# Second score pass over 128 rows, and the last norm with tokens on the partitions

## The reference

```python
def rms_norm(x, g):
    y = x * lax.rsqrt(jnp.mean(x * x, axis=-1, keepdims=True) + EPS)
    return y * g

def stick_breaking_attention(q, k, v):          # 8 heads of 64 channels
    for i in range(S // BLOCK_Q):                # blocks of 128 queries
        z = jnp.einsum('bhqd,bhkd->bhqk', qs, kk) * scale
        log_keep = jnp.where(mask, jax.nn.log_sigmoid(-z), 0.0)
        suffix = lax.cumsum(log_keep, axis=3, reverse=True) - log_keep
        a = jnp.where(mask, jnp.exp(jax.nn.log_sigmoid(z) + suffix), 0.0)
        outs.append(jnp.einsum('bhqk,bhkd->bhqd', a, vv))

def reference(x, ...):
    for l in range(DEPTH):                       # DEPTH = 2
        x = x + hybrid_mixer(x, ...)             # attention above, retention, gates, w_o
        x = x + conv_ffn(x, ...)
    return rms_norm(x, final_norm)
```

## Time and profile before

| | us |
|---|---|
| median of 3 runs | 1654.8 (1654.22 to 1655.73) |
| the profiled execution | 1654.76 |
| its span, from the first to the last instruction | 1652.9 |

### The profile page before, as it was taken

The page is one execution under the profiler, slowest core; times in us unless marked ns, Lnnn a source line. Parts: engine busy times, 40 slices in busy tenths (PEclk is TensorE's granted clock), DMA queues, the critical chain, the costliest instruction groups (busy, mean ns, idle before and its releaser), DMA issues.

```text
span 1652.9 us, 19423 instructions
## 1 busy us (share of the span) xinstructions
PE 1634.0 (99%) x7390; PEld 1351.0 (82%) x7390; DVE 943.6 (57%) x1108; ACT 638.6 (39%) x747; POOL 168.8 (10%) x157
## 2 busy tenths in 40 slices
PE   9999999999999999999999999999999999999996
PEld 7888888888888888888888888888888888888885
DVE  7268865566665566524253787645666656565223
ACT  5244334323345444522233533333333554444211
POOL 4001220000310000002200112200005000000021
PEclk9999999999999999999999999999999999999998
DMA  5332222222332323233233222232222223232321
GB/s 189 102 115 77 77 77 89 71 71 91 100 92 99 101 90 102 90 101 98 93 102 114 90 78 77 79 96 68 77 91 100 93 98 100 90 102 92 100 100 66
DMA packets 44107, 154.43 MB, mean 93 GB/s; under 512 B 4928, under 2 KB 5056, under 8 KB 44048
## 3 DMA queue, kind: packets, MB, share of 16 engines
q1 hardware_dynamic: 41904, 148.39, 27.5%
q10 hardware_dynamic: 1872, 4.33, 1.0%
q0 software_dynamic: 272, 0.85, 0.1%
HBM read 149.36 MB, written 2.10 MB: 92 GB/s over the span
## 4 chain that ended last, share of the span: by engine, by line
PE 97%; DVE 1%; DMA 0%; POOL 0%; ACT 0%; issue 0%; DVEq 0%; SPq 0%; POOLq 0%
PE ps L831 30%; PE ps L833 30%; PE ps L832 30%; PE ps L921 1%; PE ps L910 1%; PE ps L945 1%; PE ps L899 1%; PE ps L895 1%; PE ps L953 1%; PE ps L941 1%; DMA w_raw<-wts 0%; PE ps L1039 0%; PE ps L932 0%; DVE gate L821 0%; DVE rinv L818 0%; PE ps L877 0%
## 5 line engine op out<-in xcount | busy, mean ns | idle before, releaser
L831 PE MATMUL ps<-u_hi,w_hi 128*128 128x512 f32 x1344 | 530.4, 395 | 0.0
L833 PE MATMUL ps<-u_hi,w_lo 128*128 128x512 f32 x1344 | 523.6, 390 | 0.0
L832 PE MATMUL ps<-u_lo,w_hi 128*128 128x512 f32 x1344 | 523.0, 389 | 0.0
L559 DVE TENSOR_TENSOR w_lo<-w_raw,w_hi 128x1024 fp32r<-128x1024 f32 x275 | 353.4, 1294 | 289.2 <-ACT w_hi L378 285.4
L378 ACT ACTIVATE w_hi<-w_raw 128x1024 fp32r<-128x1024 f32 x275 | 288.0, 1055 | 289.4 <-DMA w_raw<-wts 283.1
L833 PEld LDWEIGHTS ps<-u_hi,w_lo 128*128 128x128 f32 x1344 | 252.3, 188 | 53.5
L831 PEld LDWEIGHTS ps<-u_hi,w_hi 128*128 128x128 f32 x1344 | 252.4, 188 | 53.2 <-issue 0.5
L832 PEld LDWEIGHTS ps<-u_lo,w_hi 128*128 128x128 f32 x1344 | 252.5, 188 | 51.7 <-issue 0.5
L831 PE MATMUL ps<-g_hi,w_hi 128*128 128x512 f32 x352 | 136.9, 389 | 0.0
L832 PE MATMUL ps<-g_lo,w_hi 128*128 128x512 f32 x352 | 136.9, 389 | 0.0
L833 PE MATMUL ps<-g_hi,w_lo 128*128 128x512 f32 x352 | 136.9, 389 | 0.0
(11 more groups left out here) (162 smaller groups left out, 1935.9 us busy)
## 6 DMA issues: line engine op xcount, KB each, us to landing
w_raw<-wts SPq DMA_DIRECT2D x275, 512.0 KB, 3.4
x<-xt SPq DMA_DIRECT2D x8, 256.0 KB, 7.2
q<-q ACTq DMA_DIRECT2D x8, 256.0 KB, 3.6
out<-gate SPq DMA_DIRECT2D x6, 256.0 KB, 2.9
dec<-decay ACTq DMA_DIRECT2D x2, 514.0 KB, 4.4
cs<-rope ACTq DMA_DIRECT2D x2, 512.0 KB, 3.8
w_raw<-wts SPq DMA_DIRECT2D x2, 256.0 KB, 4.3
out<-gate POOLq DMA_DIRECT2D x2, 256.0 KB, 3.0
```

The lines of the kernel that those rows point to most:

```text
L559: nc.vector.tensor_tensor(w_lo[:, s, :], w_raw[:, s, :], w_hi[:, s, :].bitcast(F32), ALU.subtract).then_inc(s_lo, 1)
L831: nc.tensor.matmul(dst, a_hi, b_hi, start=start, stop=False)
L832: nc.tensor.matmul(dst, a_hi, b_lo, start=False, stop=False)
L833: return nc.tensor.matmul(dst, a_lo, b_hi, start=False, stop=stop)
```

## The change

Two independent things.

The second score pass runs over 128 rows. `q_lo` becomes four tiles of 128 partitions x 2 heads x 512. Each head's low part is written to its own half of the partitions as before (line 745, now at the place `q_lo[p][b:b + 64, b // 64, :]`), and the other half holds zeros, so what it multiplies in `k2` (k's low part) adds nothing. POOL writes the zeros by four memsets in each layer, and DVE waits for them before it writes into a tile (`s_qz`). The tiles lie in parts of memory that other data use at other times, so `warm` moves too.

The last norm has tokens on the partitions. x times gain goes to `xg` (for k 0 to 3 on ACT during the last slabs, for 4 to 7 on DVE as each x is ready). PE transposes `xg` in 32 blocks of 128x128 into PSUM, four to a piece; a piece is 128 tokens x 512 channels. The sum of squares is now taken by matmuls with one column, four for `ssum`, into which POOL has added a third square, and four for the last square, so the sum stands as one column of four numbers per partition. Root and reciprocal are over 128x4 (`rcol`), and DVE and ACT in turn scale the eight pieces out of PSUM by a number per partition into `rows`. SP writes all eight, 256 KB each, in rows of 2 KB to an output whose rows are 4 KB. The host no longer transposes.

The diff:

```diff
@@ -79,7 +79,7 @@
 GR_TILE, GATE_TILE = 16, 24
 SILU_AT = 42
 SIGMOID_AT = {46: range(0, 10), 51: range(10, 16)}
-DVE_OUT = 6
+PIECES = [(0, 0), (1, 0), (2, 0), (3, 0), (1, 1), (2, 1), (3, 1), (0, 1)]
 EARLY = 2
 HALF = SLAB // 2
 WARM_UP = 8
@@ -120,8 +120,12 @@
 
         K = 1024
         x = sb("x", [P, KT, S], F32)
+        u_hi_at = at[0]
         u_hi = sb("u_hi", [P, KT, S], F32R)
+        xg = sb("xg", [P, KT, S], F32, u_hi_at)
+        u_lo_at = at[0]
         u_lo = sb("u_lo", [P, KT, S], F32R)
+        rows = sb("rows", [P, TT, D], F32, u_lo_at)
         w_hi = sb("w_hi", [P, RING, SLAB], F32R)
         ring_at = at[0]
         w_raw = sb("w_raw", [P, RING, SLAB], F32)
@@ -145,7 +149,8 @@
         TMP = M + 112 * K
         q2 = sb("q2", [P, SB_HEADS, S], F32R, QK)
         k2 = sb("k2", [P, SB_HEADS, S], F32R, G_)
-        q_lo = sb("q_lo", [P, SB_PAIRS, S], F32R, G_ + 22 * K)
+        q_lo = [sb(f"q_lo{p}", [P, 2, S], F32R, (SG_ + 12 * K, TMP + 5 * K, G_ + 22 * K, G_ + 26 * K)[p])
+                for p in range(SB_PAIRS)]
         qk_tmp = sb("qk_tmp", [P, 2, S], F32, SG_ + 8 * K)
         osb = sb("osb", [P, SB_PAIRS, 2, S], F32R, QK)
         otmp = sb("otmp", [P, S], F32, G_ + 30 * K)
@@ -179,7 +184,7 @@
         cb_at = M + 88 * K + 8 * (S + 8)
         cb = sb("cb", [P, 2, S], F32, cb_at)
         cc = sb("cc", [P, 2, S], F32, cb_at + 4 * K)
-        warm = sb("warm", [P, 512], BF16, TMP + 5 * K)
+        warm = sb("warm", [P, 512], BF16, G_ + 8 * K)
         sq = sb("sq", [P, S], F32, TMP)
         ssum = sb("ssum", [P, S], F32, TMP + 2 * K)
         assert TMP + 9 * K <= nc.sbuf_usable_end, (TMP + 9 * K, nc.sbuf_usable_end)
...
@@ -303,10 +310,13 @@
                 for i in range(SLABS // RING * RING, SLABS):
                     sp.wait_ge(s_free, l * SLABS + i + 1)
                     load(l, i % RING, i)
-            for k in range(DVE_OUT):
-                sp.wait_ge(s_fin, k + 1)
-                sp.dma_start(out[k], gate[:, k, :]).then_inc(s_out, 16)
-            sp.wait_ge(s_out, 16 * DVE_OUT)
+            for n, (tt, h) in enumerate(PIECES):
+                if n % 2 == 0:
+                    sp.wait_ge(s_find, n // 2 + 1)
+                else:
+                    sp.wait_ge(s_fina, n // 2 + 1)
+                sp.dma_start(out[tt, :, h * 512:h * 512 + 512], rows[:, tt, h * 512:h * 512 + 512]).then_inc(s_out, 16)
+            sp.wait_ge(s_out, 16 * len(PIECES))
 
         @block.gpsimd
         def _(pool):
@@ -342,6 +352,8 @@
             for l in range(DEPTH):
                 if l > 0:
                     sum_squares(l * 30, lambda k: l * TILES + k + 1)
+                for p in range(SB_PAIRS):
+                    nc.gpsimd.memset(q_lo[p][:].bitcast(F32), 0.0).then_inc(s_qz, 1)
                 for h in range(SB_HEADS):
                     pool.wait_ge(s_beta, l * 8 + h + 1)
                     for c in range(TT):
@@ -355,19 +367,10 @@
                     nc.gpsimd.tensor_tensor(rstd[:, 1, :], rstd[:, 0, :], halff, ALU.pow).then_inc(s_rs, 1)
                 sum_squares(l * 30 + 15, lambda k: l * TILES + TILE_CREDIT + WO_TILE + k + 1)
             sum_squares(DEPTH * 30, lambda k: DEPTH * TILES + k + 1, 4)
-            for k in (4, 5):
+            for k in (4, 5, 6):
                 pool.wait_ge(s_fsq, k - 3)
                 pool.wait_ge(s_sq, DEPTH * 30 + 3 + k)
                 nc.gpsimd.tensor_tensor(ssum[:], ssum[:], gate[:, KT + k, :], ALU.add).then_inc(s_sq, 1)
-
-            pool.wait_ge(s_gx, KT - DVE_OUT)
-            pool.wait_ge(s_r, DEPTH * 3 + 1)
-            for k in range(DVE_OUT, KT):
-                nc.gpsimd.tensor_tensor(gate[:, k, :], gate[:, k, :], rinv[:], ALU.mult).then_inc(s_finp, 1)
-            for k in range(DVE_OUT, KT):
-                pool.wait_ge(s_finp, k - DVE_OUT + 1)
-                pool.dma_start(out[k], gate[:, k, :]).then_inc(s_outp, 16)
-            pool.wait_ge(s_outp, 16 * (KT - DVE_OUT))
 
         @block.scalar
         def _(act):
@@ -544,11 +547,22 @@
                         for k in range(EARLY):
                             act.wait_ge(s_tile, l * TILES + TILE_CREDIT + DOWN_TILE + k + 1)
                             u_high(k, pcol(l + 1, PAR_ATTN + k))
+            nc.scalar.activation(rcol[:, 0:1], epsf, ACT.Sqrt)
+            for k in range(4):
+                act.wait_ge(s_tile, DEPTH * TILES + k + 1)
+                nc.scalar.activation(xg[:, k, :], x[:, k, :], ACT.Copy,
+                                     scale=pars[:, DEPTH * NPAR + k:DEPTH * NPAR + k + 1]).then_inc(s_xga, 1)
             for k in range(4, KT):
                 act.wait_ge(s_tile, DEPTH * TILES + k + 1)
                 nc.scalar.activation(gate[:, KT + k, :], x[:, k, :], ACT.Square).then_inc(s_fsq, 1)
             act.wait_ge(s_nrm, DEPTH * 3 + 1)
-            nc.scalar.activation(rinv[:], ps[:, 4, :], ACT.Sqrt, bias=epsf, scale=1.0 / D).then_inc(s_rt, 1)
+            nc.scalar.activation(rcol[:], ps[:, 0, 0:TT], ACT.Sqrt, bias=epsf, scale=1.0 / D).then_inc(s_rt, 1)
+            act.wait_ge(s_r, DEPTH * 3 + 1)
+            for n, (tt, h) in enumerate(PIECES):
+                if n % 2 == 1:
+                    act.wait_ge(s_xt, n + 1)
+                    nc.scalar.activation(rows[:, tt, h * 512:h * 512 + 512], ps[:, tt + 4 - 4 * h, :], ACT.Copy,
+                                         scale=rcol[:, tt:tt + 1]).then_inc(s_fina, 1)
 
         @block.vector
         def _(dve):
@@ -573,6 +587,12 @@
                 dve.wait_ge(s_oh, l * 8 + h + 1)
                 nc.vector.tensor_tensor(osb[b:b + 64, p, 1, :], otmp[b:b + 64, :], osb[b:b + 64, p, 0, :].bitcast(F32),
                                         ALU.subtract).then_inc(s_ol, 1)
+
+            def gained(k):
+
+                dve.wait_ge(s_tile, DEPTH * TILES + k + 1)
+                nc.vector.tensor_scalar(xg[:, k, :], x[:, k, :], pars[:, DEPTH * NPAR + k:DEPTH * NPAR + k + 1], None,
+                                        ALU.mult).then_inc(s_xgd, 1)
 
             def last_tile(l):
 
@@ -740,7 +760,9 @@
                                 for b in (0, 64):
                                     h = 2 * p + b // 64
                                     hi = (q2, k2)[j % 2][b:b + 64, h, :]
-                                    lo = q_lo[b:b + 64, p, :] if j % 2 == 0 else k2[64 - b:128 - b, h, :]
+                                    lo = q_lo[p][b:b + 64, b // 64, :] if j % 2 == 0 else k2[64 - b:128 - b, h, :]
+                                    if j % 2 == 0:
+                                        dve.wait_ge(s_qz, l * SB_PAIRS + p + 1)
                                     dve.wait_ge(s_qh, l * 16 + 4 * j + 2 * t + b // 64 + 1)
                                     nc.vector.tensor_tensor(lo, qk_tmp[b:b + 64, t, :], hi.bitcast(F32), ALU.subtract).then_inc(s_ql, 1)
                         if kind == "yb":
@@ -806,20 +828,21 @@
                                 slab_done(l, i)
                             nc.vector.tensor_tensor(x[:, 4 * q + t, :], x[:, 4 * q + t, :], ps[:, 4 - 4 * q + t, :],
                                                     ALU.add).then_inc(s_tile, 1)
+                            if q == 1 and l + 1 == DEPTH:
+                                gained(4 + t)
                         if q == 0 and l + 1 < DEPTH:
                             for t in range(EARLY):
                                 u_low(l * 16 + 16, t, pcol(l + 1, PAR_ATTN + t))
             last_tile(DEPTH)
-            for k in range(DVE_OUT, KT):
-                dve.wait_ge(s_tile, DEPTH * TILES + k + 1)
-                nc.vector.tensor_scalar(gate[:, k, :], x[:, k, :], pars[:, DEPTH * NPAR + k:DEPTH * NPAR + k + 1], None,
-                                        ALU.mult).then_inc(s_gx, 1)
+            gained(KT - 1)
             dve.wait_ge(s_rt, DEPTH * 3 + 1)
-            nc.vector.reciprocal(rinv[:], rinv[:]).then_inc(s_r, 1)
+            nc.vector.reciprocal(rcol[:], rcol[:]).then_inc(s_r, 1)
             dve.wait_ge(s_r, DEPTH * 3 + 1)
-            for k in range(DVE_OUT):
-                nc.vector.scalar_tensor_tensor(out=gate[:, k, :], in0=x[:, k, :], scalar=pars[:, DEPTH * NPAR + k:DEPTH * NPAR + k + 1],
-                                               in1=rinv[:], op0=ALU.mult, op1=ALU.mult).then_inc(s_fin, 1)
+            for n, (tt, h) in enumerate(PIECES):
+                if n % 2 == 0:
+                    dve.wait_ge(s_xt, n + 1)
+                    nc.vector.tensor_scalar(rows[:, tt, h * 512:h * 512 + 512], ps[:, tt + 4 - 4 * h, :], rcol[:, tt:tt + 1], None,
+                                            ALU.mult).then_inc(s_find, 1)
 
         @block.tensor
         def _(pe):
@@ -885,7 +908,7 @@
 
             def scores(l, h):
 
-                b, p = 64 * (h % 2), h // 2
+                p = h // 2
                 pe.wait_ge(s_ql, l * 16 + (6, 8, 14, 16)[p])
                 pe.wait_ge(s_qd[p // 2], l * 32 + 32)
                 if h == 0:
@@ -896,8 +919,8 @@
```

(42 more changed lines are left out.)

5 lines of the change are left out of this document (1 added, 4 removed).

## The result

The kernel after takes 1646.72 us (median of 5 runs, 1645.74 to 1647.29), the kernel before 1654.8 (5 runs, 1654.22 to 1655.93): a ratio of 0.9946 [0.9935, 0.9957], 8.1 us less. The forecast of 1645.1 has the direction right and lies 1.6 us low, inside its range of 1643.0 to 1649.5.

The account below looks back on a forecast made before the run. TensorE (PE), on the chain for 97% of the 1652.9 us span, was taken as the bound, with DMA at the end. Padding 5.2 plus end 4.5 makes 9.7 off 1654.8: 1645.1 us, own range 1643.4 to 1647, stated range 1643.0 to 1649.5.

Parts of the forecast that it names:

- The pauses: Padded second score pass: 6.4 us saved over 16 heads, less 0.8 at head 2 and 0.4 at head 3, leaves 5.2.
- the 0.40 a head: PE's scoring of each head: shorter steps and first matmuls at both borders of the second pass save 0.39, called 0.40 us.
- The steps into and out of the pass: PE at the second pass's borders: 0.26 becomes 0.12 going in, 0.25 becomes 0.12 going out, saving 0.14 and 0.13 us.
- the followers: First matmul of the pass and first weight matmul behind it: each goes from 0.34 to 0.28 us, saving 0.06.
- head 3: PE waits for DVE's sp_lo, whose chain begins with the sigmoid behind the scoring: 0.2 us lost, 0.4 in two layers.
- The end: Rebuilt last norm: first output 2.7 us earlier, then DMA bound, end of the span 4.5 us earlier; bounds 2.5 and 4.9.
- The 0.36 for POOL and DVE: Last residual adds: DVE's multiplies and POOL's adds make each other wait, releasing POOL's third add 0.36 us later; bounds 0, 1.4.
- The signs named for a right forecast: Line 922 0.12 behind line 918; 0.8 wait at head 2; root near 1634.8; eight issues within 4 us; DMA share 1.0.
- A: Scoring pauses come from the other operand or the bank, not the rows, and stay: 1650.3 us; chance 0.10.
- B: The end gives half: multiplies push back POOL's third add and SP's single queue doesn't fill the DMAs; 1647.1 us, chance 0.11.
- C: Output transfers in halves of 4 KB rows run at half DMA rate: 5.6 us more, 1650.7 us; chance 0.03.
- D: POOL's zeros slow, DVE queues behind them: memsets over 20 us begin to cost, at 24 the time is 1662.1; chance 0.02.

Follow-up runs that it names:

- alternate_64: The kernel before with the two score passes of a head alternating matmul by matmul, the second still over 64 rows; 1671.78 us.
- late_gain: The kernel after with DVE's four multiplies by the gain behind the last residual add instead of between the adds; 1646.37 us.
- alternate_128: The kernel before with only the padded second pass, the two passes alternating matmul by matmul, both over 128 rows; one run, 1651.21 us.
- part two: The kernel after with q_lo and the 64-row second pass as in before, so only the last norm is changed; 1651.55 us.
- two_queues: The kernel after with ScalarE issuing the output transfers of its own four pieces and SP only the others; 1646.69 us.
- combined: The kernel after with the changes of reorder and short_end together; 1644.52 us.
- short_end: The kernel after with POOL adding two squares, PE summing tiles 6 and 7, one piece transposed before the sums, late gain multiplies, ScalarE's piece first; 1645.17 us.
- again: The kernel after, unchanged, run and profiled once more; 1646.99 us.
- part one: The kernel before with only the padded q_lo, its memsets and the second pass over 128 rows; 1650.69 us.
- reorder: The kernel after with ScalarE's sigmoids before w_hi and DVE's scan before w_lo in the sixteen scoring slabs; 1645.57 us.
- both combined: Two kernels: combined, 1644.52 us, and combined with ScalarE issuing the output transfers of its own pieces, 1644.2 us.

## Why the prediction was right

**The pauses (5.2 forecast, 4.66 measured).** The mechanism and the 0.40 a head hold: 0.39 in each of 16 heads, 6.27 in sum. That the 0.40 came out is luck in part, by two errors that cancel. The steps into and out of the pass save 0.09 and not 0.14 and 0.13, since with 128 rows they are 0.17 and not 0.12; the followers save 0.10 each and not 0.06, since they hold their place 0.235 or near it. I had priced the quicker followers as an alternative (0.50 a head) and not taken it.

The mis-sized term is head 3: "the half saved after it (0.2) is lost". The whole 0.4 is lost. I let the chain start with the scoring, and in fact ScalarE was behind. The rows for it were in the trace of before (984.88 for the end of PE's last scoring matmul, 984.96 for the sigmoid, with `w_hi` ending at 984.93), and I didn't read them. In two layers this costs 0.4 more than forecast. The 4.66 has two further parts that the forecast knew nothing of: 0.41 lost ahead of the first scoring, and 0.45 gained in small steps between and behind the scorings, which I can't put down to anything. With them, 6.27 less 0.82 at head 2, less 0.83 at head 3, less 0.41, plus 0.45 is 4.66. From the first scoring to T alone 5.07 us are gained. That this is near 5.2 is luck too.

Of the two rules of the Trainium skill, the rows side at the borders with the one that a change of tiling mode drains TensorE ("TensorEngine Tiling (Array Packing)", section Key Properties): alternate_64 prices a border at 0.18 us. That it is a drain no row shows. The rule that a matmul over few rows takes as long as one over 128 ("TensorE: Matmul & The Clock Gate", section "Why this matters for your kernels") holds between borders: within the pass the second and third matmul hold their places 0.179 and 0.060 us with 64 rows, 0.174 and 0.061 with 128.

**The end (4.5 forecast, 4.5 measured).** Here also two terms moved against each other. The 0.36 for POOL and DVE was charged to the wrong side: POOL's adds took 1.28 to 1.30 throughout, and the multiplies were held up, 0.93, 0.80 and 0.84 instead of 0.48, each ending 0.28 behind POOL's add (1630.29 behind 1630.00). DVE's residual adds came 0.2 to 0.3 late, of which 0.05 reached POOL's third add (T + 0.70, and T + 0.65 in late_gain). So the root came 0.30 earlier than forecast. That was given back behind it: DVE's first piece starts 0.26 behind DVE's own reciprocal (ScalarE's starts 0.04 behind it, 1635.48 to 1635.52) and takes 0.75, not 0.69. The first output came at T + 5.6 as forecast, and from there to the end of the span it was 7.2 us, as forecast, with the DMA engines at 381 to 385 GB/s in the windows shown (376 assumed). That the root's 0.30 and what was given back behind it are equal is luck.

The Trainium skill's page "SBUF — State Buffer", section "Who interferes with whom", calls the shared ports an exclusive lock for a whole instruction, held by whoever came first. The traces agree in that POOL, which had started first, kept its time, and DVE's multiply ended 0.28 to 0.29 behind POOL's add, in four of four cases (three in after, one in late_gain). The row I had taken for a mutual delay (1.62 for POOL's add) misled me in its size; its DVE operation is another one, with two inputs from SBUF.

**The median.** 9.7 forecast, 9.1 in the spans, 8.1 in the medians. 0.1 went outside the span (2.0 us for after, 1.9 for before). The remaining difference lies in which executions were profiled: before's was a middle one, after's its quickest. The repeated profile, with 1.3 us more in the first slab, shows how much executions differ; that this is what separates the medians isn't shown.

**The rivals.** A fell with alternate_128. B (the end gives half) fell with the 4.5 of both profiles and of part two's own; two queues are worth 0.24, all through the earlier first issue. C (half rate for 2 KB pieces in rows of 4 KB): 381 GB/s, none of it. D: memsets of 0.95 us where 20 were needed. The signs named for a right forecast came as named, except the 0.12 (0.17) and the root at 1635.01 instead of 1634.8; the second wait of each layer grew too, by the whole 0.4.

## What to carry to other kernels

Read the starts of matmuls, not their median duration, wherever an operand of fewer rows stands between full ones: a border between 64 and 128 rows costs 0.18 us each way here, so either pad the operand with zeros or put all narrow ones in one run. Before crediting an engine with work done earlier, check that the one that takes it over is already waiting for it; its row ahead of the hand-over says so. At the end of a kernel whose outputs fill the DMA engines, count back from the last byte: what can be won is the time to the first output, and behind it nothing, as long as the later pieces stay ahead of the transfers (in combined they didn't, and 0.3 was lost).

## What the runs showed of the hardware that I had not expected

**The clock.** In after the granted clock fell from 1.00 to 0.50 (from 2.4 to 1.2 GHz) at 1636.2, in the windows above, while PE was issuing one-column matmuls and transposes without a pause since 1633.0 (11 in the microsecond before). Transposes came 0.21 apart instead of 0.11 from then on. It cost nothing in after, since the pieces stayed ahead of SP, and 0.3 in combined. What PE did just before doesn't settle when it falls: in combined and in short_end PE's matmuls from T to the first transpose behind the sums start at the same distances to 0.01, and yet the clock fell 3.4 us after T in combined and 11.8 after T in short_end. What decides it stays open.

**Two speeds of the first slab.** In some executions the first weight matmuls start 0.43 us apart instead of 0.23, until 9.0 to 10.3 us. PE's timeline of after, and of the same kernel once more, there with PE's eight warm-up matmuls ahead:

```profile
6.65 0.62 PE L900 MATMUL ps<-w_hi,u_hi 128*128 128x512 f32 x2
7.11 1.07 PE L900 MATMUL ps<-w_hi,u_lo 128*128 128x512 f32 x4
```

```profile
1.20 3.60 PE L983 MATMUL ps<-warm 128*128 128x512 bf16 x8 [1.20 <-DVE warm L602]
...
6.69 1.48 PE L900 MATMUL ps<-w_hi,u_hi 128*128 128x512 f32 x3
```

This costs 1.3 us, is never made up, and is the whole difference between the two profiles of one kernel. The windows print a granted clock of 1.00 there in both, as here for after:

```profile
7.00:8.00 1.00, 1.00 (x4) 0.71 (x4) 1.00 (x2) 0.39 (x1) 0.00 (x0) 1.00 0.89 258
```

This 1.00 says nothing so early: the view also prints it where the trace has no clock record. The first record in the packed trace, of 1.00, begins at 4.6 us in after and at 10.4 in again. In all 13 profiles it fits: it begins at 4.1 to 4.6 us in the eight whose starts are 0.23 apart, and at 9.3 to 10.4 in the five that begin with 0.43, each time inside the one step that lies between the two speeds (0.29 to 0.40 us). The warm-up matmuls, of the same 512 columns, start 0.43 apart in all 13. So the starts 0.43 apart are very likely those of the lower clock, which then lasts 5 to 6 us longer in some executions of one kernel. This is inferred, since no record covers the stretch itself. Why it lasts longer stays open; what PE did before is the same, eight warm-up matmuls from 1.2 us on.

The 0.43 was seen in the profiles of again, part two, alternate_128, late_gain and two_queues, and not in those of before, after, part one, alternate_64, reorder, short_end and both combined. These eight differ too: their first scoring slab (slab 16) begins at 95.3 to 96.2 us. The two without the padding are the earliest of them, and whether the padding has a part in this isn't shown. All this is of the size of the effects studied here, so a difference of one us between two single profiles of this kernel means nothing until its first ten are compared.
